# Moving the split of one weight half behind the root of the norm, in the GLU layers of a two-block transformer kernel

## The reference

```python
D_MODEL, SEQ, D_FF_2 = 1024, 256, 2816

def rmsnorm(x, g):
    xf = x.astype(jnp.float32)
    y = xf * lax.rsqrt(jnp.mean(xf * xf, axis=-1, keepdims=True) + EPS) * g.astype(jnp.float32)
    return y.astype(x.dtype)

def conv_glu_ffn(x, w_up, conv_w, conv_b, w_down):
    h = x @ w_up
    g, u = h[..., :D_FF_2], h[..., D_FF_2:]
    g = lax.conv_general_dilated(g, conv_w[:, None, :].astype(g.dtype), window_strides=(1,),
                                 padding=[(CONV_WIDTH_2 - 1, 0)], dimension_numbers=('NWC', 'WIO', 'NWC'),
                                 feature_group_count=D_FF_2) + conv_b
    return (jax.nn.silu(g) * u) @ w_down

# second_block, layer by layer:
#   x = x + mixed @ w_out[i]          (w_out_even, then w_out_odd)
#   x = x + conv_glu_ffn(rmsnorm(x, ffn_norm[layer]), w_up[layer], conv_w[layer], conv_b[layer], w_down[layer])
```

## Time and profile before

| | us |
|---|---|
| median of 3 executions | 1188.46 (1187.41 to 1191.78) |
| the profiled execution | 1187.41 |
| its span, first to last instruction | 1185.5 |
| PE busy in it | 1145.8 (97%) |
| DVE busy | 828.0 (70%) |
| ACT busy | 657.6 (55%) |
| mean granted clock of TensorE | 0.993 of 2.4 GHz |

### The profile page before, as it was taken

One profiled execution on the slowest core, in us unless ns is written; L12 is line 12 of the kernel. 1 busy time (PEld: TensorE's weight loads), 2 busy tenths in 40 slices (PEclk: granted clock), 3 DMA queues, 4 the chain that ended last, 5 costly groups with the idle time before them and its releaser, 6 DMA issues.

```text
span 1185.5 us, 26673 instructions
## 1 busy us (share of the span) xinstructions
PE 1145.8 (97%) x10647; PEld 977.4 (82%) x10647; DVE 828.0 (70%) x1320; ACT 657.6 (55%) x1018; POOL 133.5 (11%) x168
## 2 busy tenths in 40 slices
PE   8989999999998999999998799999999999999998
PEld 7878888888777888888876478888887778888887
DVE  7776777655785886655567749887676666977664
ACT  7564576434667466433465548655446665756432
POOL 0000200000202200000243320000123532000010
PEclk9999999999999999999999899999999999999999
DMA  8751275555361465555453416654565433765451
GB/s 335 270 197 45 95 246 201 191 192 189 135 240 61 140 239 187 204 187 192 153 179 107 143 37 223 215 200 146 179 237 183 140 122 130 252 210 181 148 181 58
DMA packets 31468, 206.59 MB, mean 174 GB/s; under 512 B 3488, under 2 KB 3872, under 8 KB 10144
## 3 DMA queue, kind: packets, MB, share of 16 engines
q1 hardware_dynamic: 31104, 205.00, 50.5%
q10 hardware_dynamic: 288, 0.52, 0.1%
HBM read 204.46 MB, written 1.05 MB: 173 GB/s over the span
## 4 chain that ended last, share of the span: by engine, by line
PE 87%; DVE 8%; ACT 2%; issue 1%; POOL 1%; DVEq 0%; ACTq 0%
PE ps L617 20%; PE ps L618 20%; PE ps L619 20%; DVE w_lo L2217 2%; PE ps L953 2%; PE ps L738 1%; PE ps L628 1%; PE ps L1380 1%; PE ps L877 1%; POOL probs L2114 1%; PE ps L853 1%; PE ps L879 1%; PE ps L878 1%; PE ps L1382 1%; PE ps L1381 1%
## 5 line engine op out<-in xcount | busy, mean ns | idle before, releaser
L1463 ACT ACTIVATE w_hi<-staged 128x2048 f16<-128x2048 f32 (+2 forms) x195 | 344.8, 1784 | 238.4 <-PE ps L619 229.4
L617 PE MATMUL ps<-f_hi,w_hi 128*128 128x256 f16 x1596 | 435.0, 273 | 0.0
L618 PE MATMUL ps<-f_lo,w_hi 128*128 128x256 f16 x1596 | 435.0, 273 | 0.0
L619 PE MATMUL ps<-f_hi,w_lo 128*128 128x256 f16 x1596 | 435.0, 273 | 0.0
L2217 DVE SCALAR_TENSOR_TENSOR w_lo<-staged,w_hi 128x2048 f16<-128x2048 f32 (+2 forms) x195 | 415.1, 2142 | 23.6 <-ACT w_hi L1463 23.5
L617 PE MATMUL ps<-x_hi,w_hi 128*128 128x256 f16 x704 | 192.0, 273 | 1.1 <-DVE tmp L2568 0.6
L619 PE MATMUL ps<-x_hi,w_lo 128*128 128x256 f16 x704 | 191.9, 273 | 0.0
L618 PE MATMUL ps<-x_lo,w_hi 128*128 128x256 f16 x704 | 191.9, 273 | 0.0
L618 PEld LDWEIGHTS ps<-f_lo,w_hi 128*128 128x128 f16 x1596 | 156.2, 98 | 19.4
L617 PEld LDWEIGHTS ps<-f_hi,w_hi 128*128 128x128 f16 x1596 | 156.2, 98 | 18.4
L619 PEld LDWEIGHTS ps<-f_hi,w_lo 128*128 128x128 f16 x1596 | 156.2, 98 | 17.9
(11 more groups left out here) (361 smaller groups left out, 1824.6 us busy)
## 6 DMA issues: line engine op xcount, KB each, us to landing
staged<-weights SPq DMA_DIRECT2D x165, 1024.0 KB, 5.2
staged<-weights SPq DMA_DIRECT2D x32, 704.0 KB, 4.3
xn<-bands SPq DMA_DIRECT2D x3, 512.0 KB, 10.1
m<-bands SPq DMA_DIRECT2D x3, 512.0 KB, 7.7
cst<-constants SPq DMA_DIRECT2D x1, 1027.0 KB, 7.9
h<-x_turned SPq DMA_DIRECT2D x2, 512.0 KB, 4.8
staged<-weights SPq DMA_DIRECT2D x2, 512.0 KB, 7.0
qT<-bands SPq DMA_DIRECT2D x2, 512.0 KB, 11.4
```

The source lines that it names most:

```text
L617: pe.matmul(out, wh, xh[:, c, :], start=(c == 0), stop=False)
L618: pe.matmul(out, wh, xl[:, c, :], start=False, stop=False)
L619: last = pe.matmul(out, wl, xh[:, c, :], start=False, stop=(c == kc - 1))
L1463: act.activation(w_hi[:, s, o:o + n], staged[:, s, o:o + n], ACT.Copy, scale=SW).then_inc(hi_split, 1)
```

## The change

Half 6 is split later, on ACT and on DVE, in both layers of the second block. On ACT its split moves from the end of `joined` to behind the root of the norm, next to the split of half 7; the wait for the sixth chunk of the output projection goes, since the wait for the eighth comes earlier now. On DVE it moves from the end of `joined_into_h` to behind pair 0, next to the split of half 7. PE, POOL and SP have the same instructions in the same order as before.

```diff
@@ joined, on ACT
                 for c in range(4, DC):
                     square(c)
-                act.wait_ge(product[name], 6)
-                split(2 * FIRST[name] + 6)
@@ glu_mlp, on ACT
                 act.activation(by_token[:, 0:1], by_token[:, 11:12], ACT.Sqrt)
                 root(f"ffn2_{layer}")
+                split(2 * FIRST[("oute", "outo")[layer]] + 6)
                 last_behind(("oute", "outo")[layer])
@@ glu_mlp, on DVE
                 pair(0, 0, (False, True))
-                split(2 * FIRST[("oute", "outo")[layer]] + 7)
+                for e in range(2):
+                    split(2 * FIRST[("oute", "outo")[layer]] + 6 + e)
                 pair(0, 1)
```

## The result

| | before | after |
|---|---|---|
| median of 7 executions, us | 1189.17 (1187.41 to 1191.78) | 1198.52 (1194.68 to 1199.81) |
| the profiled execution, us | 1187.41 | 1202.22 |
| its span, us | 1185.5 | 1200.3 |
| mean granted clock | 0.993 | 0.988 |

The ratio of the times is 1.0072, with a 95% interval of 1.0055 to 1.0088: slower, by 9.3 us between the medians. The forecast was 1195.9 us, in a range from 1191.8 to 1199.

The account below looks back on a forecast made before the run. PE's queue was taken to bound the kernel. Two stalls of 2.85 us plus one clock fall of 1.7 us gave 7.4 us on the median of 1188.46, so 1195.9 us, in a range from 1191.8 to 1199.

Parts of the forecast that it names:

- The bound: Whole kernel: PE's queue sets the end, busy 1145.8 of 1185.5 us; half 6 lies ready for 4.40 us.
- The stall: PE at the start of half 6, waiting for DVE's late split: 2.85 us in each layer, 5.7 us in all.
- The lower bound of 1.65 us: PE at half 6: the stall per layer if ACT's first tap did not come late.
- What is late next: Behind half 6: nothing found late at half 7, half 8 or the drain; a load's cover about 1.7 us thick.
- The price of a fall: TensorE's clock behind a stall: a fall to 0.59 for 4.20 us costs 1.72 us of PE's work.
- How many falls: Clock behind the two stalls: chance 0.6 each; one fall likeliest (0.48), both 0.36, none 0.16; adds 1.7 us.
- The three cases: First layer's attention: clock fell at PE's 4.7 us wait and behind 672.8 to 677.8, stayed at 1.00 around the 2.7 us wait.
- the clock would have held in both layers: Rival, behind both stalls: no fall of the clock, only 5.7 us of stalls, 1194.2 us; chance 0.15.
- a part of the stall is swallowed: Rival: second layer's attention wait absorbs 1.2 us, or each stall nears 1.65; 1191.8 us at the lower bound; chance 0.06.
- The relief on the path of the root: Rival, ACT's root and DVE's reciprocal: earlier root gains up to 1.9 us a layer, 1184.7 us; 0.03 together with no effect.
- The next cover giving way: Rival: loads after half 6 land late, ACT's split of half 10 waits; another microsecond or two a layer, 1198 to 1199; chance 0.04.

Follow-up runs that it names:

- e8: Kernel before, with only DVE's split of half 6 moved, to between the drain of chunk 0 and its taps; 1190.39 us against 1189.84, ratio 1.0004.
- e1: Kernel before with DVE's half of the change alone (half 6 split behind pair 0, ACT as before); 1192.62 us against 1188.65, ratio 1.0031.
- e2: Kernel before with ACT's half of the change alone (half 6 split behind the root, DVE as before); 1193.52 us against 1188.65, ratio 1.0037.
- e4: Changed kernel plus 24 unused PE matmuls before the wait for half 6, both layers; 1194.97 us against 1188.65 for the kernel before, ratio 1.0058.
- e3: Changed kernel with the change kept in the first layer alone; 1194.22 us against 1188.65 for the kernel before, ratio 1.0041.
- e5: The changed kernel, unaltered, run once more; 1197.14 us against 1189.84 for the kernel before, ratio 1.0070.

## Why the prediction was right

*The bound.* PE's queue sets the end, and its slack at half 6 was 4.40 us. e8 shows both: with nearly all of it used up the time is the same.

*The stall.* Forecast 2.85 us a layer, measured 2.82 in both. Each link in the first layer came as worked out: ACT's wait at the root 1.97 us (about 2.1 forecast), the first tap 1.18 us later (1.20), the rest of DVE's queue unchanged. (1.81 us less the listed wait of 0.52 would be 1.29; the prediction's 1.20 is from the starts, in which neighbouring rows of ACT overlap by 0.09.) The lower bound of 1.65 us, a stall without the late first tap, is what e1 does (1.62 and 1.69). e2 was forecast at 1.7 and measured at 1.85.

*What is late next.* Nothing: no wait of PE at halves 7 and 8, and no wait for a load. The lengths of e4 hold the bare stall (2.82 and 2.90), with no room for another term.

*The price of a fall.* Forecast 1.72 us from one row of another stage, measured 4.50 - 2.82 = 1.68. This agreement is in part luck. The trace of before has a second fall, behind the wait of 4.7 us, and it lasts twice as long:

```profile
661.10:667.90 6.80, 4.59 (x16) 2.94 (x17) 5.69 (x16) 1.43 (x4) 0.00 (x0) 0.50 0.18 35
678.20:681.60 3.40, 3.40 (x19) 1.86 (x17) 0.52 (x3) 2.60 (x10) 0.00 (x0) 0.50 0.73 277
```

The prediction took its price from the shorter one and gave no reason why the new falls should be like it. They were.

*How many falls.* This is the step that was off. I gave each stall a chance of 0.6 and took one fall as the likeliest; there were two, and five in five stalls of this kind. With two falls the sum is 2 x 2.82 + 2 x 1.68 = 9.0 us, close to the 9.3 between the medians; the forecast of 7.4 is short by one fall. (Another 0.7 us of the 2.6 between 1195.9 and the measured 1198.52 come from the kernel before, whose median is 1189.17 over seven executions and was 1188.46 over the first three.) The three cases that it was weighed from were read from one profile, and two of them come out otherwise from one profile to the next: the wait of 2.7 us near 630 us, which kept the clock in the earlier trace rows, lost it in three of the nine profiles that have it, and the two short waits near 675 us, behind which the clock fell in the earlier trace rows, brought a fall in only three of the nine. Behind the wait of 4.7 us it fell in all nine. One profile of a wait whose outcome varies is poor evidence for a chance. By the rule of the Trainium skill's page "TensorE: Matmul & The Clock Gate" (section "Part 1: The HAM clock gate") the clock would have held in both layers, and the change would have cost 5.6 us; the traces disagree, five times in five.

*The rivals.* That a part of the stall is swallowed: shown wrong by e3. The relief on the path of the root: ACT's margin of 0.17 us there grew to 1.97 and no one gained by it. The next cover giving way: no sign of it in any profile.

Open: why a wait of 2.7 us at 630 us lost the clock in three profiles of nine and one of the same length at half 6 in five of five. The stretches around them differ in what PE does there, and no run tells apart what of that counts.

## What to carry to other kernels

Where one engine's queue sets the end, reordering the others can at best do nothing, unless it takes work from ahead of something that engine waits for. So compare when each input is ready with when it is taken, and follow the moved step through every queue that it passes, for here the late first tap of another engine added 1.2 us to the move. A stall of the bounding TensorE of 2.8 us cost 4.5, since the clock fell behind it in each of the five cases; work that nobody needs, put in front of a wait that can't be avoided, takes that second part away. And compare stretches between two fixed points of the profiles rather than whole times where the start varies by more than the effect.

## What the runs showed of the hardware that was not expected

- The clock can fall after PE has begun again: in the first profile PE ran at the full rate for some time from 734.06 on before the low level came; in e5 it was low from the first matmul of half 6 on (listed at 0.39 us and not 0.28). The loss was nearly the same, 1.7 us against 1.6.
- None of four stalls of 1.45 and 1.67 us brought a fall, and each of the five of 2.65 us at the same place did.
- The same wait with the same length can lose the clock in one execution and keep it in the next (lost in three of nine near 630 us, and in three of nine near 675 us), and the time goes with it: the stretch of the first layer's attention, which nine of the kernels share, took 137.6 to 138.0 us with the one fall that all nine have, 139.0 to 139.7 with one more and 140.6 with two more.
